# Prompt attention with its eight query tiles in the order 0, 7, 1, 6, 2, 5, 3, 4

## The reference

```python
o_cmp, p_cmp = attend_shared(q, ck, cv, cend[None, :] <= qpos[:, None])      # 63 compressed keys
...                                        # the 16 best of 16 blocks of 64 tokens: all of them
o_sel = attend_gathered(q, k_sel, v_sel, kpos <= qpos[None, :, None, None])  # causal, all keys so far
wmask = ((kwpos[None, :] >= 0) & (kwpos[None, :] <= qpos[:, None])
         & (kwpos[None, :] > qpos[:, None] - WINDOW))                        # causal, last 512 keys
o_win, _ = attend_shared(q, kw, vw, wmask)
o = gn[..., 0:1] * o_cmp + gn[..., 1:2] * o_sel + gn[..., 2:3] * o_win
```

## Time and profile before

| | us |
|---|---|
| three runs: lowest, median, highest | 2221.97, 2226.47, 2227.95 |
| the profiled execution's own time | 2227.64 |
| its span, from first to last instruction | 2226.0 |
| the stage, from the first cmp scores to the last output copy | 639.8 to 900.1 |

### The profile page before, as it was taken

The page is one execution under the profiler, slowest core; times in us unless marked ns, Lnnn a source line. Parts: engine busy times, 40 slices in busy tenths (PEclk is TensorE's granted clock), DMA queues, the critical chain, the costliest instruction groups (busy, mean ns, idle before and its releaser), DMA issues. The chain is left out here.

```text
span 2226.0 us, 38457 instructions
## 1 busy us (share of the span) xinstructions
PE 2124.0 (95%) x14076; PEld 1970.4 (89%) x14076; DVE 928.1 (42%) x1958; ACT 551.5 (25%) x1151; POOL 616.5 (28%) x539
## 2 busy tenths in 40 slices
PE   7999999978989999789999998999999999999998
PEld 7999999955855767589999987999999999999997
DVE  4111111176326676454662346563333333333335
ACT  5001211112326656221130332131111111111112
POOL 2233332335314444422112322121212222121220
PEclk9999999989979999899999999999999999999999
DMA  6112222485314000553312422120111102111121
GB/s 197 55 47 66 68 95 88 118 231 174 101 50 140 9 1 2 133 149 111 116 38 76 190 81 91 38 67 28 57 38 52 52 29 66 31 54 47 33 62 78
DMA packets 210807, 175.77 MB, mean 79 GB/s; under 512 B 25931, under 2 KB 191531, under 8 KB 210122
## 3 DMA queue, kind: packets, MB, share of 16 engines
q1 hardware_dynamic: 203306, 155.02, 23.0%
q0 software_dynamic: 5024, 10.69, 1.8%
q10 hardware_dynamic: 2368, 8.67, 1.0%
HBM read 147.02 MB, written 27.39 MB: 78 GB/s over the span
## 5 line engine op out<-in xcount | busy, mean ns | idle before, releaser
L152 POOL TENSOR_TENSOR tail_w_lo<-mem_last_slot,tail_w_hi 128x1024 fp32r<-128x1024 f32 (+1 forms) x94 | 183.5, 1952 | 689.8 <-ACT tail_w_hi L140 689.8
L191 PE MATMUL ff_psum<-tail_hi,tail_w_hi 128*128 128x352 f32 x1056 | 341.2, 323 | 1.0 <-PEq L2108 1.0
L192 PE MATMUL ff_psum<-tail_lo,tail_w_hi 128*128 128x352 f32 x1056 | 338.5, 321 | 0.0
L193 PE MATMUL ff_psum<-tail_hi,tail_w_lo 128*128 128x352 f32 x1056 | 338.2, 320 | 0.0
L191 PE MATMUL bank<-mix_hi,in_w_hi 128*128 128x352 f32 x840 | 272.0, 324 | 0.0
L192 PE MATMUL bank<-mix_lo,in_w_hi 128*128 128x352 f32 x840 | 270.0, 321 | 0.0
L193 PE MATMUL bank<-mix_hi,in_w_lo 128*128 128x352 f32 x840 | 269.8, 321 | 0.0
L140 ACT CAST tail_w_hi<-mem_last_slot 128x1024 fp32r<-128x1024 f32 (+1 forms) x94 | 81.2, 863 | 509.5 <-PE ff_psum L193 433.4
L191 PEld LDWEIGHTS ff_psum<-tail_hi,tail_w_hi 128*128 128x128 f32 x1056 | 198.1, 188 | 1.9 <-issue 1.5
L192 PEld LDWEIGHTS ff_psum<-tail_lo,tail_w_hi 128*128 128x128 f32 x1056 | 198.4, 188 | 0.1
L193 PEld LDWEIGHTS ff_psum<-tail_hi,tail_w_lo 128*128 128x128 f32 x1056 | 197.9, 187 | 0.0
(11 more groups left out here) (393 smaller groups left out, 3837.0 us busy)
## 6 DMA issues: line engine op xcount, KB each, us to landing
in_raw<-w_in SPq DMA_DIRECT2D x70, 256.0 KB, 3.2
mem_last_slot<-w_gate SPq DMA_DIRECT2D x44, 256.0 KB, 3.2
mem_last_slot<-w_up SPq DMA_DIRECT2D x44, 256.0 KB, 3.3
mem_last_slot<-w_down SPq DMA_DIRECT2D x80, 128.0 KB, 2.2
gate_kept<-x_first ACTq DMA_DIRECT2D x16, 528.0 KB, 2.7
uv<-gate_kept SPq DMA_DIRECT2D x16, 528.0 KB, 4.7
mem_ring<-cache_mem_v SPq DMA_DIRECT2D x8, 1024.0 KB, 14.1
mem_ring<-cache_mem_k SPq DMA_DIRECT2D x7, 1024.0 KB, 7.2
```

Source lines behind the costliest of these rows:

```text
L152: pool.tensor_tensor(lo, raw, hi.bitcast(F32), ALU.subtract).then_inc(self.split, 1)
L191: pe.matmul(out, hi, x_hi, start=k == 0, stop=False)
L192: pe.matmul(out, hi, x_lo, start=False, stop=False)
L193: last = pe.matmul(out, lo, x_hi, start=False, stop=k == len(terms) - 1)
```

## The change

The tile that stands in place t is no longer tile t but `TILES[t]`. Every use of the tile's number as data (queries, keys in reach, masks, gates, output columns, block counts) goes through the table. Places still count the buffers' parity, the semaphores and the ring. The wait for the window mask moves to the place where the mask is first used, place 1. One blank line and the table's line shift the line numbers behind them by 1 and by 2 or 3; the prediction uses those of before.

```diff
+        TILES = (0, 7, 1, 6, 2, 5, 3, 4)
         def blocks(u):
-            t, _, kind = units[u]
-            return G if kind == "cmp" else t + 1 if kind == "sel" else min(t + 1, 5)
+            tile, kind = TILES[units[u][0]], units[u][2]
+            return G if kind == "cmp" else tile + 1 if kind == "sel" else min(tile + 1, 5)
...
-                        pool.tensor_scalar(pr, pr, factor[:, u % 4, h:h + 1], gates[:, t, j:j + 1], ALU.mult, ALU.mult).then_inc(normed, 1)
+                        pool.tensor_scalar(pr, pr, factor[:, u % 4, h:h + 1], gates[:, TILES[t], j:j + 1], ALU.mult, ALU.mult).then_inc(normed, 1)
...
-                    qt = slice(t * P, t * P + P)
-                    k0 = 0 if kind != "win" else max(t - 4, 0) * P
+                    qt = slice(TILES[t] * P, TILES[t] * P + P)
+                    k0 = 0 if kind != "win" else max(TILES[t] - 4, 0) * P
...
-                    k0 = 0 if kind == "sel" else max(t - 4, 0)
+                    k0 = 0 if kind == "sel" else max(TILES[t] - 4, 0)
...
-                    act.copy(oT[:, g, t * P:(t + 1) * P], out[g % 2][:, 0:P]).then_inc(out_kept, 1)
+                    act.copy(oT[:, g, TILES[t] * P:(TILES[t] + 1) * P], out[g % 2][:, 0:P]).then_inc(out_kept, 1)
...
-                                          hidden[:, t].unsqueeze(1).to_broadcast([P, 8, CMP]), ALU.add).then_inc(lowered, 1)
+                                          hidden[:, TILES[t]].unsqueeze(1).to_broadcast([P, 8, CMP]), ALU.add).then_inc(lowered, 1)
...
-                    mask = window if kind == "win" and t >= 4 else causal[:, NP - n:NP]
-                    if kind == "win" and t == 4:
+                    mask = window if kind == "win" and TILES[t] >= 4 else causal[:, NP - n:NP]
+                    if kind == "win" and t == 1:
                         dve.wait_ge(window_in, 16)
...
-                        gate = gates[:, t, :].rearrange("p (h g j) -> p g h j", h=2, g=4)[:, :, :, 0]
+                        gate = gates[:, TILES[t], :].rearrange("p (h g j) -> p g h j", h=2, g=4)[:, :, :, 0]
```

## The result

| | before | after |
|---|---|---|
| median of 20 runs each | 2224.57 us | 2230.23 us |
| lowest to highest | 2221.97 to 2229.54 | 2224.47 to 2233.18 |
| the profiled execution's span | 2226.0 | 2228.1 |
| the stage, from the first cmp scores to the last output copy | 639.80 to 900.09: 260.3 | 638.57 to 903.53: 265.0 |

The ratio of the two is 1.0021, with a 95% interval of 1.0014 to 1.0029: the new order is slower by 0.2%, 3.1 to 6.5 us, inside the 0.3% that I had called no change. The stage is 4.7 us longer in the trace, as much as the ratio says of the whole. The spans of these two executions differ by 2.1 only: this one reached the stage 1.2 us earlier and took 1.3 us less behind it, where nothing was changed.

A forecast was written before the change was run, and what follows sets the result against it. PE's own instructions were taken to bound the steady stage, with waits only at tile changes. Waits after 7.8 + 2.4 = 10.2, less 7.0 before, plus 0.3 at the end, gave +3.5: 2226.47 + 3.5 = 2230.0 us, range 2223 to 2238.

The forecast's parts named there:

- The work, the start and SP cost nothing: PE's total work, tile 0's start with its slow clock, and SP's loads: all unchanged, 0 us.
- The pace of the pairs stays: One sel plus one win unit inside a tile keeps its time wherever the tile stands: 8.71 us tile 5, 9.35 tile 6.
- Waits before, 7.0 us: PE's waits at tile starts in the old order: 6.0 us in six tiles and about 1.0 for tile 7.
- Short to long, 7.8 us: Waits at changes 0 to 7, 1 to 6, 2 to 5, 3 to 4: 2.4, 2.4, 2.0 and 1.0 us.
- Long to short, 2.4 us: Waits at changes 7 to 1, 6 to 2, 5 to 3: 0.8 us each; bounds 0 and 6.0.
- the neighbours: All changes between tiles: waits of 10.2 us after against 7.0 before.
- Parity, nothing beyond 0.4 us a tile: Swapped copying engines in tiles 6 and 4: nothing in steady pairs; 0.4 us at the start, within the waits already taken.
- The end, +0.3: Stage drains with tile 4, whose last sel unit waits 0.77 us in place of 0.44: 0.3 us more.
- a second stretch at half the clock: Sign of a wrong forecast: the clock at 0.5 again, where 1.00 was expected from 666 on.
- the mix fills the short tiles: Rival: tiles 1, 2 and 3 take 4.5, 5.1 and 2.1 us less; -11.7, time 2215; chance 0.05.
- DVE becomes the bound: Rival: late DVE copies in tiles 6 and 4 add 9.2 us to 3.5; time 2239; chance 0.14.
- The clock falls again: Rival: a wait at change 0 to 7 starts tile 7 at half rate, up to 9 us; time 2239; chance 0.05.

The follow-up runs named there:

- a: New order 0, 7, 1, 6, 2, 5, 3, 4, with each tile's copying engines as in the kernel before; stage 261.7 us, ratio 1.0001.
- f: Kernel after, with the reciprocal for sel and win units put ahead of the copy on VectorE; stage 255.7 us, ratio 0.9974 to the kernel before.
- m: Order 0, 7, 2, 5, 4, 3, 6, 1, each tile's best copying engines, reciprocal ahead of the copy; stage 249.6 us, ratio 0.9957 to kernel before.
- d: Kernel before in order 0, 7, 2, 5, 4, 3, 6, 1, copying engines unchanged in every tile; stage 258.2 us, ratio 0.9994.
- k: Kernel after, unchanged, in a second profiled execution; stage 264.9 us.
- i: Order of d with the best copying engines in each tile; stage 252.3 us, ratio 0.9959 to the kernel before.
- b: Kernel before in its old order, with the copying engines each tile had in the kernel after; stage 268.4 us, ratio 1.0048.
- c: Kernel before, but VectorE copies first groups in tiles 0 to 3, ScalarE the 4-block groups in tiles 4 to 7; stage 256.5 us, ratio 0.9988.
- e: Kernel before, with the reciprocal for sel and win units put ahead of the copy on VectorE; stage 255.8 us, ratio 0.9989.
- h: Old order with the copying engines of c and the reciprocal ahead of the copy; stage 254.5 us, ratio 0.9971 to the kernel before.

## Why the prediction came out right, step by step

The time was right (2230.0 forecast, 2230.23 measured), and so was the stage (about 264 forecast, 265.0 measured). That the time fits to 0.2 us is luck: the forecast started from a median of 2226.47 of three runs, 1.9 us above the 2224.57 of twenty, and the change itself was 4.7 us by the ratio, not 3.5. Nor was the sum right for its reasons; two terms were mis-sized, in opposite directions, and the clock was left out of it.

- **The work, the start and SP cost nothing.** Right: PE has the same 14076 instructions, and up to unit 9 nothing differs.
- **The pace of the pairs stays.** Right in tiles 5 and 6 (8.69 and 9.34 us) and 7, but not in tile 1, 4.45 in place of 4.23, nor quite in tile 4, 8.15 in place of 8.05. And the reading behind it, that the even pace in the blocks is PE's own in every tile, was wrong for the short ones: with the reciprocal moved a pair of tile 1 takes 4.03 us and one of tile 2 5.33 in place of 5.55.
- **Waits before, 7.0 us.** Too low: they are 8.8. I had taken the cmp unit as 1.8 us with hardly a wait in it, and so tiles 3 and 4 as having 0 and 0.2 us of waits; their rows give 0.9 and 0.8. The 1.0 for tile 7 was a guess, and right (0.97).
- **Short to long, 7.8 us.** The rows of the kernel after give 2.6 for tile 7 (forecast 2.4), 2.5 for tile 6 (2.4), 2.3 for tile 5 (2.0) and 1.7 for tile 4 (1.0): 9.1. With the old copies (a) tiles 6 and 4 have 1.9 and 0.8, which makes 7.5.
- **Long to short, 2.4 us.** With the old copies 1.7; with the new ones 2.3.
- **So the neighbours** cost 1.4 us by run a, with the fall of the clock in it, which alone is worth 1.8; I had said 10.2 - 7.0 = 3.2. This term was sized too high, mostly through the base.
- **Parity, nothing beyond 0.4 us a tile.** This is the step that failed. It costs 3.3 us, after against a. I looked at it only where one group is larger than the other (tiles 4 and 6) and asked whether DVE would be full. The cost is a delay, not load: DVE is busy 76% of tile 6, not 86%. Tiles 1 and 3, whose groups are equal, pay 0.6 and 0.9 us; the 0.6 and about half of the 0.9 are there because the reciprocal stands behind the later of the two copies, as f shows. I had named that loop in the section on the kernel, and then priced it only at a tile's first units. Tiles 6 and 4 pay 1.0 each where I allowed 0.4, and in them most of it stays when the reciprocal is moved: it goes with the copy of 4 blocks, 0.69 us on DVE against 0.58 on ACT, in the first wait, in the pairs and, in tile 4, in the three waits at the end.
- **The end, +0.3.** Right for the waits: three of 0.77.

One of my own signs of being wrong came true: a second stretch at half the clock. Of the rivals, "the mix fills the short tiles" did not come: tile 1 got longer. But there was room: m takes 10.7 us out of the stage; the order alone does not reach it. That this is near the 11.7 that I had worked out for the rival is in part chance, since 1.8 of it is at the stage's end and 1.8 in tile 0 (22.8 us against 24.6 in d, the same order), which the rival did not count. The rule of the Trainium skill on weight loads ("Perfetto Trace Analysis", Identifying the Most-Contended Engine) pointed to that room, and there the trace agrees with it more than with my reading of the pace: the pair of 4.03 us. "DVE becomes the bound" did not come in that form: the only steady sign is the 0.1 us in the pairs of tile 4. "The clock falls again" did come, at the place that I named, with a chance of only 0.05 given to it; only its price was wrong, 1.8 us in place of up to 9, since the clock was back after 3.4 us and not 18. The trace agrees there with the Trainium skill ("TensorE: Matmul & The Clock Gate", HAM oscillation) in that waits between bursts of matmuls can throttle the clock again; here one of 1.27 us was followed by a fall in four executions (after, a, d, k), and in f, i and m by none.

## What to carry to other kernels

A new order of equal work is not only an order: whatever is handed out by a running count's parity (buffers, engines) changes hands with it. To learn what the order itself is worth, keep each tile's assignment (a), and give the order back with the new assignment (b); the two runs together say which it was. And in a hand-written pipeline a small instruction that another engine waits for, such as a reciprocal, goes ahead of a copy that itself waits: here that took 4.5 us off the stage of the old order in the trace (0.4 to 4.7 us by the times). And a stage's length from one execution has chance in it: where the clock happens to stand when the stage starts moved it by 0.9 us here.

## What the runs showed of the hardware that I had not expected

The granted clock does not simply stay up once it is up. In tile 0 or just behind it, it fell to half for 3 to 7 us in 8 of the 14 traced kernels and executions of this stage (after, a, b, c, d, e, h, k), each time behind waits of PE of 0.2 to 1.3 us and without any long stop. The two longest, 6.8 us each, were in b, where PE had done nothing in 2.75 of 8 us, and in e, where it had just waited 1.13 us. And in the kernel before it stayed at half from the stage's start to 666.0, although PE was busy for 88% of tile 0; in the six kernels with a quicker tile 0 (c, e, f, h, i, m) it was back at full 22.3 to 23.7 us after the stage's start, in the other eight executions after 25.7 to 26.5. So the clock adds to what an edit of tile 0 gains or loses.
